# Three FFN chunk pairs in seven block products instead of two, with weight sums and FoX masks added by accumulating DMAs

## The reference

```
a, b = split(h @ w_in)            # w_in: 1024 x 5632, w_out: 2816 x 1024
x = x + 0.5 * (silu(a) * b) @ w_out
```

## Time and profile before

| | |
|---|---|
| time, median of 3 runs | 1044.06 us (1043.92 to 1044.14) |
| the profiled execution's own time | 1042.84 us |
| its span, first to last instruction | 1041.1 us |
| PE, DVE, ACT, POOL busy | 99%, 74%, 56%, 15% |
| mean granted TensorE clock | 0.997 |
| moved by DMA | 182.78 MB, 176 GB/s |

### The profile page before, as it was taken

One profiled execution on the slowest core, in us unless ns is written; L12 is line 12 of the kernel. 1 busy time (PEld: TensorE's weight loads), 2 busy tenths in 40 slices (PEclk: granted clock), 3 DMA queues, 4 the chain that ended last, 5 costly groups with the idle time before them and its releaser, 6 DMA issues.

```text
span 1041.1 us, 13003 instructions
## 1 busy us (share of the span) xinstructions
PE 1028.7 (99%) x5076; PEld 847.2 (81%) x5076; DVE 765.6 (74%) x925; ACT 587.4 (56%) x732; POOL 151.6 (15%) x140
## 2 busy tenths in 40 slices
PE   8999999999999999999999999999999999999997
PEld 7888888888888888788888888788888888878886
DVE  6897875677576579868656769868766657986864
ACT  6565454656476565555456555546446656555543
POOL 3613111000013150000000150000470015000000
PEclk9999999999999999999999999999999999999999
DMA  9919456457401492742746692752646149274261
GB/s 307 340 23 375 151 155 224 144 181 216 148 2 41 123 341 61 273 171 82 228 145 194 220 345 83 252 193 81 206 158 202 42 141 341 64 269 175 82 202 41
DMA packets 112349, 182.78 MB, mean 176 GB/s; under 512 B 5960, under 2 KB 67504, under 8 KB 112160
## 3 DMA queue, kind: packets, MB, share of 16 engines
...
...
q10 hardware_dynamic: 176, 0.05, 0.0%
...
## 4 chain that ended last, share of the span: by engine, by line
PE 92%; DVE 4%; issue 2%; ACT 1%; DMA 0%; ACTq 0%; DVEq 0%
PE acc L571 13%; PE acc L573 13%; PE acc L572 13%; PE inb L571 12%; PE inb L573 12%; PE inb L572 12%; PE acc L837 2%; PE inb L864 2%; PE tb L849 2%; PE tb L572 1%; PE tb L573 1%; PE tb L571 1%; PE tb L706 1%; DVE wlo L1586 1%; PE inb L861 1%
## 5 line engine op out<-in xcount | busy, mean ns | idle before, releaser
L1586 DVE TENSOR_TENSOR wlo<-raw,whi 128x2048 fp32r<-128x2048 f32 x131 | 319.8, 2443 | 107.9 <-ACT whi L1154 107.7
L1154 ACT CAST whi<-raw 128x2048 fp32r<-128x2048 f32 x131 | 250.5, 1915 | 52.3 <-PE inb L573 19.9
L571 PE MATMUL inb<-whi,thi 128*128 128x512 f32 x528 | 210.1, 398 | 0.6 <-DVE work L1751 0.6
L573 PE MATMUL inb<-whi,tlo 128*128 128x512 f32 x528 | 206.2, 391 | 0.0
L572 PE MATMUL inb<-wlo,thi 128*128 128x512 f32 x528 | 205.9, 390 | 0.0
L571 PE MATMUL acc<-whi,fhi 128*128 128x512 f32 (+1 forms) x384 | 149.0, 388 | 0.0
L573 PE MATMUL acc<-whi,flo 128*128 128x512 f32 (+1 forms) x384 | 148.3, 386 | 0.0
L572 PE MATMUL acc<-wlo,fhi 128*128 128x512 f32 (+1 forms) x384 | 148.2, 386 | 0.0
L571 PEld LDWEIGHTS inb<-whi,thi 128*128 128x128 f32 x528 | 99.3, 188 | 21.4 <-issue 2.2
L573 PEld LDWEIGHTS inb<-whi,tlo 128*128 128x128 f32 x528 | 99.2, 188 | 21.2
L572 PEld LDWEIGHTS inb<-wlo,thi 128*128 128x128 f32 x528 | 99.4, 188 | 19.4
...
## 6 DMA issues: line engine op xcount, KB each, us to landing
...
```

What stands on the lines that cost most here:

```text
L571: pe.matmul(o, lh, rh, start=start, stop=False, skip_group_check=True)
L573: return pe.matmul(o, ll, rh, start=False, stop=stop, skip_group_check=True)
L1154: act.copy(whi[u % RING][:, :], unit_source(u)).then_inc(s_hi, 1)
L1586: dve.tensor_tensor(wlo[u % RING][:, :], unit_source(u), whi[u % RING][:, :].bitcast(F32), ALU.subtract).then_inc(s_lo, 1)
```

## The change

Each FFN now runs three pairs and five plain chunks, `"nnnsnsns"`; the pairs are chunks 3/4, 6/7 and 9/10. Between two pairs stands one plain chunk, and the third pair ends the FFN. There PE turns the first token half between M7 and M4 and the second half in the middle of the last unit's first token half. Signs are arranged so that the weights' combinations are sums: t1 = B11 + B12, t3 = B22 + B12, t2 = t1 + B22, t4 = t2 + B21. B11 is loaded twice, once through the ring (unit M1) and once into `sum_a`; B22 twice, into `sum_b` and `work`. POOL then issues two DMAs that read B12 from DRAM and add it to `sum_a` and `sum_b`. t2 and t4 stay on DVE. The first load of the next pair waits until M4 of the pair before is split. The token sums move from POOL to DVE (POOL still joins), bias rows and FoX's c from POOL to ACT, FoX's masks to two accumulating DMAs with 512-byte pieces. The bias loads of the first FFN move to its end.

The core of the diff, lines left out where the text above says it:

```diff
-KINDS = "nnnsnnsnn"
+PLAIN = ("a", "b", "o", "M1")
+KINDS = "nnnsnsns"
...
-            return {"M1": b11, "M2": b21, "M3": b22, "M5": x, "M6": b11, "M7": b12, "M4": x}[kind]
+            return {"M2": b21, "M3": b22, "M5": sum_a, "M6": sum_a, "M7": sum_b, "M4": sum_a}[kind]
...
-                    u = b + UNIT_OF["M7", PAIRS[n - 1]]
-                    sp.wait_ge(s_tw, 4 * (len(PAIRS) * f + n))
+                    u = b + UNIT_OF["M4", PAIRS[n - 1]]
+                    sp.wait_ge(s_tw, 2 * (len(PAIRS) * f + n))
                     sp.wait_ge(s_lo, u + 1)
                 if i == 0:
-                    pair_in(f, j, 0, 0, b11, s_b11)
+                    pair_in(f, j, 0, 0, sum_a, s_la)
                 elif i == 1:
-                    pair_in(f, j, 0, 1, b12, s_b12)
+                    pair_in(f, j, 1, 1, sum_b, s_lb)
                 elif i == 2:
...
+                    elif kind == "M1":
+                        r = raw[LOADS[u][0]][:, :].rearrange("p (k n) -> p k n", k=4)
+                        w = ffn_w_in[f // 2, f % 2][0:512, j * FC:j * FC + CW].rearrange("(k p) n -> p k n", p=P)
+                        load(u, [(r[:, k:k + 2], w[:, k:k + 2]) for k in (0, 2)])
                     if n < len(PAIRS) and (kind, j) == (("o", 0) if n == 0 else ("b", PAIRS[n - 1] + 2)):
                         i = 0
-                    if i is not None and kind in "abo":
+                    if i is not None and kind in PLAIN:
...
                 product(f, j, "M7", "S3", inb[0], False, True)
+                if j == LAST_ROWS[0]:
+                    pair_turn(f, j, 0)
                 pe.wait_ge(s_c12, n)
                 product(f, j, "M4", "A22", tb[1], True, True)
-                pair_turn(f, j, 0)
+                if j != LAST_ROWS[0]:
+                    pair_turn(f, j, 0)
 
...
                 pe.wait_ge(s_lo, u + 1)
+                pe.wait_ge(s_glo, NTURNS * f + turns_before(j) + 1)
                 for k in range(2):
                     for n in range(2):
                         out_columns(u, j, 0, n, k)
                 pe.wait_ge(s_lo, u + 2)
+                out_last(u + 1, last, 0, lambda: pair_turn(f, j, 1))
                 pe.wait_ge(s_glo, NTURNS * f + NTURNS)
-                out_last(u + 1, last, 0)
                 for n in range(2):
                     out_columns(u, j, 1, n, 0)
                 if following:
...
+                    n = len(PAIRS) * f + PAIRS.index(j) + 1
+                    ready = {"M2": (s_b21, 32 * n), "M3": (s_b22, 32 * n), "M5": (s_t1, 16 * n), "M7": (s_t3, 16 * n),
+                             "M6": (s_tw, 2 * n - 1), "M4": (s_tw, 2 * n)}
+                    act.wait_ge(*ready[kind])
...
+                if f == 2:
+                    decays(j, 0)
+                elif f == 0:
+                    bias_rows(j, 0)
...
+            def bias_rows(j, i):
+
+                if j not in (1, 2):
+                    return
+                act.wait_ge(s_setup, 2)
+                starts = bucket_starts()
+                half = 2 * (j - 1) + i
+                for b in range(NB // 4 * half, NB // 4 * (half + 1)):
+                    near, far = starts[b], starts[b + 1] - 1
+                    ins = act.copy(rows[:, SEQ - 1 - far:SEQ - near], tbT[:, b:b + 1].broadcast_to([H, far - near + 1]))
+                ins.then_inc(s_rows, 1)
+
+            def decays(j, i):
+
+                where = {1: 1, 2: 1, PAIRS[0] + 2: 0, PAIRS[1] + 2: 0}
+                if j not in where:
+                    return
+                t, half = where[j], 2 * (j in (2, PAIRS[1] + 2)) + i
+                act.wait_ge(s_cq, 1)
+                act.wait_ge(s_mask1 if t else s_mask0, 16)
+                for h in range(4 * half, 4 * half + 4):
+                    d = bias[:, h, :] if t else decay0[:, h, :]
+                    ins = act.activation(d, d, ACT.Identity, bias=cq[:, t, h:h + 1])
+                ins.then_inc(s_decay, 1)
...
+            def token_sums(f):
+
+                m = whole_tokens(f)
+                dve.wait_ge(s_whole, 2 * f + 2)
+                dve.wait_ge(s_rc, f + 1)
+                for t in range(NT):
+                    tok = slice(t * P, (t + 1) * P)
+                    dve.tensor_tensor(m[:, :, tok], m[:, :, tok],
+                                      rstd_row[:, tok].unsqueeze(1).broadcast_to([P, KT, P]),
+                                      ALU.mult).then_inc(s_an, 1)
+                dve.wait_ge(s_an, 2 * f + 2)
+                a11, a12, a21, a22 = [quarter(m, a) for a in ("A11", "A12", "A21", "A22")]
+                dve.tensor_tensor(four(c22), a21, a22, ALU.subtract).then_inc(s_as, 1)
+                dve.wait_ge(s_as, 4 * f + 1)
+                dve.tensor_tensor(a21, a11, a21, ALU.subtract).then_inc(s_as, 1)
+                dve.wait_ge(s_as, 4 * f + 2)
+                dve.tensor_tensor(a11, four(c22), a11, ALU.subtract).then_inc(s_as, 1)
+                dve.wait_ge(s_as, 4 * f + 3)
+                dve.tensor_tensor(a12, a12, a11, ALU.add).then_inc(s_as, 1)
+
+            def t2_weights(f, j):
 
                 n = len(PAIRS) * f + PAIRS.index(j) + 1
                 dve.wait_ge(s_b22, 32 * n)
-                dve.wait_ge(s_tw, 4 * n - 3)
-                dve.tensor_tensor(b12, b22, b12, ALU.subtract).then_inc(s_tw, 1)
-
-            def t2_weights(f, j):
-
-                n = len(PAIRS) * f + PAIRS.index(j) + 1
-                dve.wait_ge(s_tw, 4 * n - 2)
-                dve.tensor_tensor(b11, b12, b11, ALU.add).then_inc(s_tw, 1)
+                dve.tensor_tensor(sum_a, sum_a, b22, ALU.add).then_inc(s_tw, 1)
 
             def t4_weights(f, j):
 
                 n = len(PAIRS) * f + PAIRS.index(j) + 1
                 dve.wait_ge(s_b21, 32 * n)
-                dve.wait_ge(s_tw, 4 * n - 1)
-                dve.tensor_tensor(combined(f), b21, b11, ALU.subtract).then_inc(s_tw, 1)
+                dve.tensor_tensor(sum_a, sum_a, b21, ALU.add).then_inc(s_tw, 1)
...
                 if pair == PAIRS[0]:
                     for name in SPLITS:
                         tokens_lo(f, name)
-                if pair:
-                    t1_weights(f, pair)
                 lo(a + 3)
                 dve.wait_ge(s_gt, NTURNS * f + turns_before(j))
                 for t in range(NT):
                     hidden_tile(2 * (NSEG * f + i) + t, t)
-                if pair:
-                    t3_weights(f, pair)
                 lo(a + 4)
                 for r in rows:
                     u = b + UNIT_OF["o", r]
...
                 lo(m["M1"] + 3)
+                lo(m["M5"] + 3)
                 t4_weights(f, j)
-                lo(m["M5"] + 3)
                 lo(m["M5"] + 4)
...
-                dve.tensor_tensor(c12, tb[1][:, :], c12, ALU.add).then_inc(s_c12, 1)
+                dve.tensor_tensor(c12, tb[1][:, :], c12, ALU.subtract).then_inc(s_c12, 1)
                 dve.wait_ge(s_c12, n)
                 dve.wait_ge(s_silu, 2 * (NSEG * f + i) + 1)
                 dve.tensor_tensor(c12, c12, sa_p, ALU.mult).then_inc(s_g, 1)
                 lo(m["M3"] + 3)
+                if j == LAST_ROWS[0]:
+                    pair_hidden_lo(f, j, 0)
                 dve.wait_ge(s_used, m["M7"] + 1)
                 dve.tensor_tensor(u3, inb[0][:, :], u3, ALU.add).then_inc(s_u3, 1)
                 dve.wait_ge(s_u3, n)
-                dve.wait_ge(s_m5, n)
-                dve.tensor_tensor(c22, c22, u3, ALU.add).then_inc(s_c22, 1)
-                lo(m["M7"] + 3)
-                pair_hidden_lo(f, j, 0)
+                if j == LAST_ROWS[0]:
+                    lo(m["M7"] + 3)
+                else:
+                    dve.wait_ge(s_m5, n)
+                    dve.tensor_tensor(c22, c22, u3, ALU.subtract).then_inc(s_c22, 1)
+                    lo(m["M7"] + 3)
+                    pair_hidden_lo(f, j, 0)
                 dve.wait_ge(s_used, m["M4"] + 1)
-                dve.scalar_tensor_tensor(out=u3, in0=tb[1][:, :], scalar=rstd[:, 1:2], in1=u3, op0=ALU.mult,
+                c21 = c12 if j == LAST_ROWS[0] else u3
+                dve.scalar_tensor_tensor(out=c21, in0=tb[1][:, :], scalar=rstd[:, 1:2], in1=u3, op0=ALU.mult,
                                          op1=ALU.add).then_inc(s_c21, 1)
+                if j == LAST_ROWS[0]:
+                    dve.wait_ge(s_m5, n)
+                    dve.tensor_tensor(c22, c22, u3, ALU.subtract).then_inc(s_c22, 1)
                 dve.wait_ge(s_c22, n)
                 dve.wait_ge(s_silu, 2 * (NSEG * f + i) + 2)
                 dve.tensor_tensor(c22, c22, sa_p, ALU.mult).then_inc(s_g, 1)
-                lo(m["M4"] + 3)
+                if j != LAST_ROWS[0]:
+                    lo(m["M4"] + 3)
...
+                pair_hidden_lo(f, LAST_ROWS[0], 1)
+                ffn_add(f, 0)
                 lo(b + FFN_UNITS)
-                ffn_add(f, 0)
...
+            def add_blocks(f, n):
+
+                j, m = PAIRS[n], len(PAIRS) * f + n + 1
```

(66 more changed lines are left out.)

69 lines of the change are left out of this document (30 added, 39 removed).

## The result

The changed kernel takes 1132.32 us (median of 4 runs, 1130.98 to 1133.49), the kernel before 1043.99; the ratio is 1.0847, 95% interval 1.0833 to 1.0861. It was forecast slower, at 1073 us, and it is 59 us slower than that, outside the range.

The account below looks back on a forecast made before the run. PE was taken to bound the kernel, every wait paid in full. Saved product -9.2, FFN ends +4.0 and waits between pairs +34 gave +29 us on 1042.84, 1072; the runs' median 1.2 above, so 1073 us, range 1036 to 1094.

Parts of the forecast that it names:

- hold nothing back: Rival: the accumulating DMAs do not delay unit o's block between pairs, so no waits there; 1039 us, chance 0.27.
- The saved product: Seven products for eight in a third pair per FFN: 2.3 us saved an FFN, -9.2 us in all.
- the FFN's end: With a pair last, PE waits at both token-half turns and for splitting: 1.0 us an FFN, +4.0 us.
- c = 1.5: Ratio of an accumulating DMA's engine time to a plain load's, taken as 1.5 with bounds 1.0 and 3.
- The layout of the blocks: SP's queue between pairs, with landing times; o of chunk 4 sixth, landing at 444.2 alone, 452.0 with adds.
- Three moves where a load makes two: Reason given for 1.5: an accumulate reads two operands and writes one, against a plain load's two moves.
- The eight places: Both later pairs of every FFN, where PE waits for M1 and unit o: 4.3 us each, +34 us.
- The 1094 us given beside that 51: Total stated for an add ratio of 1.9 from the skill page, with some 51 us of waits between pairs.
- the first pair of an FFN loads over several chunks; nothing for them: Claim that the adds cause no waits at each FFN's first pair: 0 us.
- The rival of a doubled add (1094): Rival: an add costs a full second load or more, 6.9 us a place between pairs; 1094 us, chance 0.15.
- What costs nothing: Token sums on DVE, bias rows and FoX's c on ACT, mask DMAs: hidden, at most one wait of a few us.

Follow-up runs that it names:

- The long artificial stalls: The kernel before with PE made to wait 12 times ahead of a unit o for seven POOL memsets and a small one: 1121.30 us, ratio 1.0743.
- the short ones: The kernel before with PE made to wait 12 times ahead of a unit o for one 512-column POOL memset and a small one: 1057.84 us, ratio 1.0132.

## Why the prediction was wrong

**The way and the cause were right.** The adds' engine time pushes M1 and unit o, and PE waits at the turn and at unit o. Without the adds the time is 1038.06, where the rival "hold nothing back" had 1039.

**The saved product and the FFN's end** (-9.2 and +4.0) came out at -6.9 together by the run without adds and -6 by the third pair's own worth, where -5.2 stood. The turns at the end wait 1.0 + 1.0 = 2.0 us in four FFNs, in place of 4.0; the 0.7 us on DVE's L1803 is the wait behind the first pair that the kernel before has as well.

**First failed step: c = 1.5.** The layout of the blocks was sound. Measured from SP's gate it had M1 landing after 16.2, 17.2 and 18.2 us with c at 1, 1.5 and 2, and unit o after 24.6, 27.2 and 29.8. Seen, by the start of ACT's casts, were 18.3 and 30.05, and M1 alone, by its 1.7 + 4 x 2.6 + 2.0, at 14.1, which is what the run without adds shows to the tenth. So c is 2, and the engine time of add and copy (5.6 against 2.7 us) says 2.1 by another way. "Three moves where a load makes two" had no row behind it; packets and engine time both double. The eight places wait 5.0 to 6.7 us apiece in PE's timeline, in all 47.0 us, where 34 stood; the layout's own price for c = 2 was 6.9 a place, 55, so it was 8 us too dear there. The price worked out from the Trainium skill, "Collectives: The Full Stack", bandwidth ceiling, was 51; the trace agrees with it better than with the 34 that was taken. The 1094 us given beside that 51 doesn't add up: 1044.1 - 5.2 + 51 is 1090, and 1094 belongs to 55.

**Second: "the first pair of an FFN loads over several chunks; nothing for them".** Their waits are 3.7, 3.4, 6.0 and 3.4 us, 16.5 in all. The loads do spread, but the two adds go out as soon as each block lands, in the third FFN at 654.40 and 660.08, and the ring load that SP had issued at 652.67, behind sum_b's block, reaches ACT at 673.08, after 11.7 us of idleness:

```profile
673.08 1.90 ACT L1165 CAST whi<-raw 128x2048 fp32r<-128x2048 f32 x1 [11.74 <-DMA raw<-in_ffn_w_in]
```

**Third, the largest: a stall was priced at its length.** PE is under way 31.7 us longer than without the adds. The long artificial stalls cost 2.1 us each beyond their wait, the short ones 0.3. An estimate from these: fourteen of the 22 stalls with a lowered clock behind them at 2.1 us and eight without at 0.3 make 31.8. Nothing in the kernel before showed it, since its PE never waits that long.

The sum mended: -6.9 + 47.0 + 16.5 + 31.7 = 88.3 us on 1044.0, 1132.3. This is an account of two traces, not a second forecast that came true. The rival of a doubled add (1094) had the first of these terms about right, 55 for 47, and was short by the other two.

**What costs nothing** held: two pairs with all these edits differ from the kernel before by a ratio of 1.0008.

**What stays open.** Between 1.87 and 2.44 us the length alone doesn't tell which stalls a lowered clock follows: 2.13 us before 533.09 was followed by 1.00, 1.87 us before 475.64 by 0.66 in the 5 us behind it. No run looked for what decides it. With the adds kept, one other order was tried, and not the second add moved by itself.
